# First layer of a three-layer float32 block: the four pooled products placed between whole tiles, and the weight stream laid out to match

## The reference

```python
def even_mixer(h, w_in, sink, w_pool, pool_scale, w_out):
    z = h @ w_in                                  # 1024 x 1280
    q, k, v, u = split(z)                         # 512, 128, 128, 512 columns
    q = rope(q); k = rope(k)
    ya = windowed_gqa(q, k, v, sink)              # 8 heads of 64, keys |i-j| <= 128
    yb = multiscale_pool(u, w_pool, pool_scale)   # 4 groups of 128 channels
    return concatenate([ya, yb]) @ w_out          # 1024 x 1024

# multiscale_pool, for group g with window w = 2, 4, 8, 16:
#   d = (sum of u over w positions) / count - u ;  y_g = (d @ w_pool[g]) * pool_scale
```

## Time and profile before

| | |
|---|---|
| median of three runs | 1613.89 us (1612.09 to 1614.36) |
| profiled execution, its own time | 1611.82 us |
| span of its trace | 1610.0 us |
| TensorE busy | 1489.6 us, 93% |
| VectorE busy | 783.1 us, 49% |
| mean granted TensorE clock | 0.969 of full |

### The profile page before, as it was taken

One profiled execution on the slowest core, in us unless ns is written; L12 is line 12 of the kernel. 1 busy time (PEld: TensorE's weight loads), 2 busy tenths in 40 slices (PEclk: granted clock), 3 DMA queues, 4 the chain that ended last, 5 costly groups with the idle time before them and its releaser, 6 DMA issues.

```text
span 1610.0 us, 20388 instructions
## 1 busy us (share of the span) xinstructions
PE 1489.6 (93%) x7110; PEld 1167.8 (73%) x7110; DVE 783.1 (49%) x1417; ACT 622.9 (39%) x1126; POOL 566.1 (35%) x236
## 2 busy tenths in 40 slices
PE   6979899999999987788999999999989799899997
PEld 5657678888888866545778888888867677666785
DVE  6783442223444677586333223444466236476434
ACT  4443332232323456545433232232353234655432
POOL 4222254444444433100235444444423352122441
PEclk9999999999999988979999999999989999899998
DMA  5212232322223221100123232332322232111221
GB/s 215 68 51 66 66 105 91 102 94 96 100 91 103 70 89 66 53 1 1 61 76 112 91 104 92 99 97 91 104 66 79 92 107 77 40 53 53 66 79 53
DMA packets 36624, 129.55 MB, mean 80 GB/s; under 512 B 4048, under 2 KB 4176, under 8 KB 36560
## 3 DMA queue, kind: packets, MB, share of 16 engines
q1 hardware_dynamic: 35136, 124.80, 23.7%
q10 hardware_dynamic: 1424, 3.90, 0.7%
HBM read 126.58 MB, written 2.10 MB: 80 GB/s over the span
## 4 chain that ended last, share of the span: by engine, by line
issue 58%; POOL 22%; PE 16%; DVE 2%; ACT 1%; POOLq 1%; DVEq 0%; ACTq 0%
POOL w L558 22%; PE bank L575 4%; PE bank L577 4%; PE bank L576 4%; PE bank L698 1%; PE bank L712 1%; PE bank L680 1%; DVE arena L1996 0%; POOLq L557 0%; POOLq L555 0%; ACT tmp L1114 0%; ACT tmp L1104 0%; DVE arena L1628 0%; DVE arena L1886 0%; ACT arena L1383 0%
## 5 line engine op out<-in xcount | busy, mean ns | idle before, releaser
L558 POOL TENSOR_TENSOR w<-raw,w 128x1024 fp32r<-128x1024 f32 x232 | 565.9, 2442 | 1010.8 <-ACT w L1048 628.2
L575 PE MATMUL bank<-opC,w 128*128 128x512 f32 x624 | 255.3, 409 | 26.0 <-POOL w L558 14.2
L577 PE MATMUL bank<-opC,w 128*128 128x512 f32 x624 | 246.8, 395 | 0.0
L576 PE MATMUL bank<-opC,w 128*128 128x512 f32 x624 | 246.4, 395 | 0.0
L1604 DVE TENSOR_TENSOR mlp_op<-arena,mlp_op 128x512 fp32r<-128x512 f32 x64 | 144.5, 2260 | 188.7 <-ACT mlp_op L1171 188.7
L575 PE MATMUL bank<-mlp_op,w 128*128 128x512 f32 x560 | 221.5, 396 | 10.0 <-DVE arena L1516 9.5
L1143 ACT ACTIVATE w<-raw 128x1024 fp32r<-128x1024 f32 x126 | 133.2, 1057 | 239.5 <-PE bank L577 239.5
L576 PE MATMUL bank<-mlp_op,w 128*128 128x512 f32 x560 | 220.5, 394 | 0.0
L577 PE MATMUL bank<-mlp_op,w 128*128 128x512 f32 x560 | 220.3, 393 | 0.0
L575 PE MATMUL bank<-opA,w 128*128 128x512 f32 x428 | 168.8, 394 | 6.8 <-ACT arena L1317 2.3
L577 PE MATMUL bank<-opA,w 128*128 128x512 f32 x428 | 167.4, 391 | 0.0
(11 more groups left out here) (213 smaller groups left out, 1928.2 us busy)
## 6 DMA issues: line engine op xcount, KB each, us to landing
raw<-stream_dram SPq DMA_DIRECT2D x232, 512.0 KB, 3.4
out_t_dram<-arena SPq DMA_DIRECT2D x8, 256.0 KB, 2.1
x<-x_t_dram SPq DMA_DIRECT2D x4, 256.0 KB, 5.7
x<-x_t_dram ACTq DMA_DIRECT2D x4, 256.0 KB, 7.2
rope<-ropes_dram ACTq DMA_DIRECT2D x2, 512.0 KB, 6.8
con<-consts_dram ACTq DMA_DIRECT2D x1, 993.5 KB, 8.2
arena<-p_t_dram ACTq DMA_DIRECT2D x1, 512.0 KB, 4.2
par<-params_dram ACTq DMA_DIRECT2D x1, 253.5 KB, 3.8
```

The costliest lines, as they stand in the source:

```text
L558: pool.tensor_tensor(w_lo[:, j, :], raw[:, j, :], w_hi[:, j, :].bitcast(F32), ALU.subtract).then_inc(lo_made, 1)
L575: pe.matmul(out, wh, hi, start=first, stop=False)
L576: pe.matmul(out, wh, lo, start=False, stop=False)
L577: return pe.matmul(out, wl, hi, start=False, stop=last)
```

## The change

The fills get one list of tiles, `E_TILES`, in which the four pool tiles no longer follow the ten of the input projection but stand among them. The stream holds the sub-blocks of these 22 tiles one behind the other with no padding between, so that a tile may begin in the middle of a block; it has as many blocks as before (17 for this part). The number of products by step changes too: before 5 in steps 0 to 9, 4 in step 10, 6 in steps 11 to 16, 5 in 17 and 18; now 5 in 0 to 9, 6 in 10 to 16, 4 in 17 and 18. The places in `SPLITS` follow. The rule for banks is the old one, by tile number.

```diff
-EIN = [4, 0, 5, 1, 6, 7, 2, 8, 9, 3]
-BESIDE_EVEN = ("ein", "pool", "eout_a")
+E_TILES = ([("ein", i) for i in (4, 0, 5, 1, 6, 7)] + [("pool", 0), ("ein", 2), ("pool", 1), ("ein", 8), ("ein", 9), ("pool", 2),
+           ("ein", 3), ("pool", 3)] + [("out", m) for m in range(KT)])
+E_COUNT = {"ein": KT, "pool": 1, "out": len(OUT_EARLY)}
...
-STAGES = [("ein", 10, 8), ("pool", 4, 1), ("eout_a", 8, len(OUT_EARLY)), ("eout", 8, len(OUT_LATE)), ("up0", 32, 8), ("down0", 8, 32),
+STAGES = [("ein", len(E_TILES), 6), ("eout", 8, len(OUT_LATE)), ("up0", 32, 8), ("down0", 8, 32),
...
-SPLITS = [("even", 8), ("pool", (0, 1)), ("eattn", (0,)), ("pool", (2, 3)), ("pooled", (0, 1)),
-          ("eattn", (1,)), ("pooled", (2, 3)), ("eattn", (2, 3)), ("mlp0", 8), ("odd", 8), ("xc", 4),
+SPLITS = [("even", 8), ("pool", (0, 1)), ("pooled", (0, 1)), ("eattn", (0,)), ("pool", (2, 3)), ("pooled", (2,)),
+          ("eattn", (1,)), ("pooled", (3,)), ("eattn", (2, 3)), ("mlp0", 8), ("odd", 8), ("xc", 4),
...
 def e_pace(step):
 
-    return 5 if step < 10 else 4 if step == 10 else 6 if step < 17 else 5
+    return 5 if step < 10 else 6 if step < 17 else 4
...
-            def e_product(stage, i, k):
-
-                t, count = TILE0[stage] + i, {a: n for a, _, n in STAGES}[stage]
-                s = SUB0[stage] + i * count + k
+            def e_product(kind, i, k, s):
+
+                t = e_tile(kind, i)
                 if k == 0 and t >= 4:
                     pe.wait_ge(z_ready, t - 1)
                 if s % SUBS == 0 or k == 0:
                     pe.wait_ge(lo_made, s // SUBS + 1)
...
-                for stage, i in E_DONE[s]:
-                    if stage == "eout_a":
-                        residual_tile("eout_a", i)
-                    elif stage == "pool":
+                for kind, i in E_DONE[s]:
+                    if kind == "out":
+                        residual_tile("out", i)
+                    elif kind == "pool":
                         src = taken("pool", i)
                         TS(pooled_y[i], src[:, :], g("pool_scale", i), None, ALU.mult).then_inc(z_ready, 1)
```

More of the change, by code:

```diff
@@ L145, in block_ends @@
             for i in range(tiles):
-                s += k if name != "ple" else (8, 2)[i % 2]
+                s += E_COUNT[E_TILES[i][0]] if name == "ein" else k if name != "ple" else (8, 2)[i % 2]
                 ends[s - 1] = t + i + 1
-        end = SUB0[name] + tiles * k
+        end = SUB0[name] + (sum(E_COUNT[kind] for kind, _ in E_TILES) if name == "ein" else tiles * k)
         for b in range(SUB0[name] // SUBS, -(-end // SUBS)):
@@ L229, in e_work @@
 def e_work():
-    out = [(stage, i, k) for stage in BESIDE_EVEN for i in range(NTILES[stage])
-           for k in range({a: n for a, _, n in STAGES}[stage])]
+    out, s = [], 0
+    for kind, i in E_TILES:
+        for k in range(E_COUNT[kind]):
+            out.append((kind, i, k, s))
+            s += 1
     return out[SUBS * HEAD + E_AHEAD:]
 def e_pace(step):
-    return 5 if step < 10 else 4 if step == 10 else 6 if step < 17 else 5
+    return 5 if step < 10 else 6 if step < 17 else 4
 def e_steps(n_steps):
@@ L244, in e_steps @@
     ends = HEAD + E_AHEAD // SUBS
+    last = work[-1]
     for step in range(n_steps):
         events = []
[L247 to L252, removed]
+        for item in work[at:at + e_pace(step)]:
+            kind, i, k, s = item
+            if k == E_COUNT[kind] - 1:
+                events.append((kind, i))
+            ends += s % SUBS == SUBS - 1 or item == last
         at += e_pace(step)
@@ L1509, in taken @@
                     return bank[OUT2_BANKS[i % 4]]
-                if name in BESIDE_EVEN and t >= HEAD:
+                if name in E_COUNT and t >= HEAD:
                     return bank[6 + t % 2]
@@ L2043, in weight_stream @@
     order = lambda which: [i if name == "eattn" else 4 + i for name, i in which]
-    out.append(padded(eout[:, order(OUT_EARLY)]))
+    tiles = dict(ein=sub_blocks(a["e_w_in"][0], ein), pool=a["e_w_pool"][0][:, None], out=eout[:, order(OUT_EARLY)])
+    out.append(padded(np.concatenate([tiles[kind][i] for kind, i in E_TILES])))
     out.append(padded(eout[:, order(OUT_LATE)]))
```

57 lines of the change are left out of this document (28 added, 29 removed).

## The result

The changed kernel took 1619.47 us (median of 16 runs, 1616.03 to 1623.51), the kernel before 1614.82 us on the same chips (16 runs, 1611.95 to 1620.43). The ratio is 1.0025, 95% interval 1.0014 to 1.0037: slower by 4.0 us in 1614.8 by the ratio and by 4.65 us between the medians, where the forecast had +4.0. The measured time lies inside the forecast's range (1612 to 1622.5), 1.6 us above its value of 1617.9.

A forecast was written before the change was run, and what follows sets the result against it. TensorE, 93% busy, was taken as the bound. Waits and starts summed to +1.9 us and one more clock fall to +2.1, so +4.0 on 1613.9 gave 1617.9 us, range 1612 to 1622.5.

The forecast's parts named there:

- Step 3: Input projection fill: TensorE waits 3.4 us for bank 7 behind pool product 0; 0.55 us before step 4's scores goes; net 2.8.
- Step 7: Before the rotation: the wait for the finished heads' low part grows from 2.57 to 3.9 us, net 1.4 us.
- Steps 8 to 10: Waits of 0.3, 0.5 and 0.9 us before scores, values and output projection's first tile: net -1.2 us, between -2.9 and +1.5.
- Step 11: Head of the fill: one 3.3 us wait for pooled result 3's low part replaces 2.34 and 1.61 us, net -0.7 us.
- Starts: Five small gaps fewer on TensorE save their start-up, some 0.1 us each: -0.4 us.
- The clock: Gaps of 3.4, 3.9 and 3.3 us bring two falls of TensorE's clock, one more than before: +2.1 us.
- Layout: Weight stream: as many blocks as before, made three ahead as before, so the weights cost nothing.
- the first (fewer falls): Rival: same waits, but the clock falls once or not at all, +1.9 or -0.2 us, 1615.8 or 1613.7 us; chance 37%.
- The second: Rival: GpSimd goes first in step 11, whose wait grows by 2.5 to 5.8 us: +6.5 us, 1620.4 us; chance 6%.
- The third, faster: Rival: the gaps of steps 8 to 11 vanish wholly: -5.2 us, 1608.7 us; chance 12%.

The follow-up runs named there:

- the first experiment: Changed kernel with pool tiles 0 and 1 side by side behind input tile 2: 1617.17 us, ratio 1.0014 to the kernel before.
- the moved block: Changed kernel with the weight block that step 2 makes ready made in step 3 instead (ScalarE edit): one run, 1617.55 us.
- the old pace: Changed kernel with the old products by step (4 in step 10, 5 in steps 17 and 18): 1618.21 us, ratio 1.0012 to the kernel before.
- layout alone: Contiguous stream with the old tile order, `SPLITS` and products by step: 1614.17 us against 1616.57 of the kernel before, ratio 0.9984.
- the run with the delayed block: Changed kernel with ScalarE making no weight block ready in step 3 and two in step 4: one run, 1620.6 us.
- heads first: Changed kernel with the finished heads' low part made ahead of taking out tile 8 in VectorE's step 6: 1613.71 us, ratio 0.9999 to the kernel before.
- before, both lists: Kernel before with two VectorE edits: heads' low part first in step 6, step 11's rotation behind the pooled low parts. 1613.18 us, ratio 0.9981.
- before, heads only: Kernel before with only the heads' low part made first in VectorE's step 6: one run, 1617.75 us.
- all four edits: Changed kernel with pool tiles paired, heads' low part first, step 11's rotation behind the low part, old products by step: 1605.38 us, ratio 0.9935 to before.

## Why the prediction was right

**Step 3**: forecast 3.4 us for bank 7 less 0.55, net 2.8; measured 3.20 less 0.55, net 2.65. The new order of tiles in the first experiment removed exactly this wait, which shows the bank as its cause, and the moved block shows that 1.55 us of it were GpSimd's. By the rule cited from the Trainium skill (SBUF — State Buffer, Who interferes with whom) the scaling is held for GpSimd's whole instruction; the run with the moved block agrees, 0.75 us in place of 2.30.

**Step 7**: forecast 3.9 us, measured 3.93; net 1.36 for 1.4.

**Steps 8 to 10**: forecast 0.3, 0.5 and 0.9 us, measured 0.50, 0.37 and 0.67; net -1.56 for -1.2, since GpSimd's block fell into the windows as said (4.22 us for three sums; the whole window work took 6.0 us for the forecast's 5.7), and VectorE had caught up with it nevertheless.

**Step 11**: forecast 3.3 us (5.13 less 1.9 is 3.2), measured 3.13; net -0.8 for -0.7. The sentence that the two moved products "come to no more and no less" holds for their own time only. The step's term had their effect in it (first product of the fill and not the third), but put it down to nothing in particular; the old pace shows that 1.4 us of the wait were the pace's doing, 1.0 us net, and could have been had separately.

**Starts**: the -0.4 us for fewer small gaps did not show; 117.7 and 117.6 us are left before and after. Waits alone: +1.6 us for the forecast's +1.9.

**The clock**: the step that was mis-sized. Forecast were two falls at 2.1 us against one at 2.1; measured three at 1.7 against one at 2.6, +2.5 for +2.1. That the two errors nearly cancel is luck: a fall was taken to be of one length, and it isn't. It is luck too that the total fits. The traced execution of the kernel before was one of its quickest and lost 49.9 us to the clock, against 53.3 on average; over all runs the clock adds 0.9 us (54.2 against 53.3) and not one whole fall, and the rest adds 2.8 us, where the forecast had 1.9 for the waits. The two traces have 3.0 us for it: 1.6 of waits, 0.6 for the later start, and 0.8 that counts here since half of the 1.61 us that TensorE stood within the long fall was booked as lost to the clock. The rule of the Trainium skill (TensorE: Matmul & The Clock Gate, HAM oscillation), that gaps between bursts bring the slow clock back, bore on the profiled execution: all three long waits were followed by a fall, where the prediction had taken two. The kernels with the same waits and other falls show that it can't be counted on for a single gap.

**Layout**: that the blocks are made three ahead and so the weights cost nothing is right for TensorE, which never waited for a block. But it left out that a block which ends at another step puts GpSimd's 2.4 us beside other work of VectorE. The layout alone took away 1.8 us of waits in its trace, though its ten runs show only 0.4 us less at full clock than the kernel before. In the changed kernel it can show in step 11 no more, as the pair was already gone there.

**Rivals**: the first (fewer falls) did not come in the profiled execution, and none of the changed kernel's 16 runs had a higher granted clock over the whole program than the traced one's 0.968. The second did not come: 0.36 us of lead. The third, faster, needed the waits of steps 8 to 11 to go, and step 11's could not, as the rotation stood ahead of it. Moving that rotation took 1.93 of the 3.13 us away, and the old pace 1.4. The scores of step 11 stood at 120.33 us; forecast were 116.6 and 2.1 for each of the two falls by then, 120.8. Two errors meet here as well: the falls took 1.7 us each, and everything began 0.6 us later than before, which the forecast did not have.

## What to carry to other kernels

When tiles alternate between two banks, a one-product tile between whole ones leaves the next tile waiting for the tile just ended. Place it so that other work, here the attention part of the next step, stands before the tile that wants that bank; pairing the short tiles does not do it by itself. Read which instruction ends each wait of the bounding engine and move that instruction forward in its own engine's list, then look at what another engine holds up beside it. Here four changes of nothing but order (two in VectorE's lists, one of the tiles, one of the pace), with no work removed, turned a change that cost 0.25% into one that gains 0.65%. Moving a wait by one edit can bring it back a step later, as on the kernel before, so judge edits of an order together and by a stretch, not by the wait that goes.

## What the runs showed of the hardware

The lower clock level comes after gaps, but not after each, and not at fixed places. With waits the same to 0.01 us, the changed kernel's clock fell behind the gaps of 3.20, 3.93 and 3.13 us, and in the run with the delayed block at the last two only, the first of these falls twice as long. With heads first, the 3.13 us brought none. Falls of 3.4 us also stood at 45 us, behind the first scores' wait of 2.2 us, in four kernels ("before, both lists", "layout alone", "block in step 3" and "before, heads only"), and in the others not, with the same wait. The first scores of these four started at 44.13 to 44.28 us, those of all others at 44.65 us or later.

Runs of one kernel spread with the clock. Of the 82 runs of the kernel before, the ten with a granted clock of 0.969 over the program took 1612.0 to 1612.7 us, the 43 with 0.967 took 1614.0 to 1617.3, and the two with 0.963 took 1621.2 and 1623.8; 1 us more lost to the clock came with 1.0 us more of span. A stretch without a fall does not make the whole steady: all four edits ran at 0.970 each time and took 1604.1 to 1606.2 us, and with the moved block, equally without a fall in the stretch, the clock was 0.969 to 0.971 and the times 1602.5 to 1607.8 us. Where in the program the falls of the untraced runs lie is not known.

VectorE's operations with their inputs in SBUF alone were held for GpSimd's whole instruction: the scaling, 2.30 us in place of 0.75 for two; a window sum, 2.60 in place of 0.71; a pair of low parts, 3.45 in place of 1.29; a single low part, 2.84 in place of 0.69. Which operation pays depends on where the weight block falls, and a block moved by one step was worth 1.55 us on TensorE's path.
